# Low parts of the selecting stage's u tiles from an accumulating DMA instead of VectorE, heads of two engines unrolled

## The reference, cut to what matters

```python
q  = (h @ w_pq).reshape(b, s, PEER_HEADS, 2, PEER_HALF)          # 8 heads
sc = einsum('bshpc,pnc->bshpn', q, sub_keys)                     # 2 x 128 keys
top_v, top_i = lax.top_k(sc, 16)                                 # per half
cand = top_v[..., 0, :, None] + top_v[..., 1, None, :]
best_v, best_i = lax.top_k(cand, 16)
expert = i1 * 128 + i2                                           # of 16384 experts
gate = softmax(best_v)
a   = einsum('bthkd,btd->bthk', u_emb[expert], h)
out = einsum('bthk,bthkd->btd', gelu(a) * gate, v_emb[expert])
```

## Time and profile before

| | us |
|---|---|
| median of 3 runs | 4106.17 |
| lowest, highest | 4091.32, 4109.74 |
| the profiled execution's own time | 4093.63 |
| its span in the trace | 4091.9 |
| selecting, about | from 1657 to 2693 |

### The profile page before, as it was taken

One profiled execution on the slowest core, in us unless ns is written; L12 is line 12 of the kernel. 1 busy time (PEld: TensorE's weight loads), 2 busy tenths in 40 slices (PEclk: granted clock), 3 DMA queues, 4 the chain that ended last, 5 costly groups with the idle time before them and its releaser, 6 DMA issues. The chain is left out here.

```text
span 4091.9 us, 62946 instructions
## 1 busy us (share of the span) xinstructions
PE 3733.3 (91%) x21687; PEld 3298.7 (81%) x21687; DVE 3030.5 (74%) x5237; ACT 1466.2 (36%) x2548; POOL 1670.7 (41%) x1277
## 2 busy tenths in 40 slices
PE   6999999998899999799888889888886999999997
PEld 5776777775677877698888888888886999999996
DVE  5677777777753413469999999784463999999998
ACT  3455555566543433322222222233342222222222
POOL 2433434443212112025555555632222656566562
PEclk9999999998999999899999999989997999999998
DMA  2111111111343313158888888845448999999995
GB/s 86 44 52 47 52 41 48 47 50 65 123 181 113 113 36 115 53 190 309 307 290 317 316 316 308 320 173 219 167 152 329 387 390 389 387 391 387 388 391 201
DMA packets 316060, 848.09 MB, mean 207 GB/s; under 512 B 28752, under 2 KB 124240, under 8 KB 311888
## 3 DMA queue, kind: packets, MB, share of 16 engines
q1 hardware_dynamic: 202384, 400.92, 28.7%
q0 software_dynamic: 110592, 402.70, 25.9%
q10 hardware_dynamic: 2880, 41.94, 2.5%
HBM read 726.96 MB, written 118.49 MB: 207 GB/s over the span
## 5 line engine op out<-in xcount | busy, mean ns | idle before, releaser
L1922 POOL DMA_INDIRECT join_urow<-in_u_rows,select_row_now x384 | 510.8, 1330 | 510.7 <-issue 244.9
L2652 POOL DMA_INDIRECT spread_vrow<-in_v_rows,spread_row_of x384 | 543.3, 1415 | 379.3 <-DVE spread_y L2723 263.6
L163 PE MATMUL spread_banks<-spread_ahi,spread_vhi 128*128 128x384 f32 (+1 forms) x2048 | 638.0, 312 | 35.7 <-DVE spread_acc L2713 20.9
L163 PE MATMUL select_products<-h_hi,shared_pair_hi 128*128 128x256 f32 (+2 forms) x1728 | 575.6, 333 | 98.5 <-DVE shared_raw_low L1736 89.0
L164 PE MATMUL spread_banks<-spread_alo,spread_vhi 128*128 128x384 f32 (+1 forms) x2048 | 635.1, 310 | 0.0
L165 PE MATMUL spread_banks<-spread_ahi,spread_vlo 128*128 128x384 f32 (+1 forms) x2048 | 634.9, 310 | 0.0
L163 PE MATMUL shared_carry<-shared_wide_hi,shared_w_hi 128*128 128x512 f32 x1408 | 559.4, 397 | 28.6 <-DVE shared_wide_lo L591 11.2
L164 PE MATMUL select_products<-h_lo,shared_pair_hi 128*128 128x256 f32 (+2 forms) x1728 | 569.8, 330 | 2.8 <-issue 2.8
L165 PE MATMUL select_products<-h_hi,shared_raw_low 128*128 128x256 f32 (+2 forms) x1728 | 569.5, 330 | 2.2 <-issue 2.1
L164 PE MATMUL shared_carry<-shared_wide_lo,shared_w_hi 128*128 128x512 f32 x1408 | 554.8, 394 | 0.0
L165 PE MATMUL shared_carry<-shared_wide_hi,shared_w_lo 128*128 128x512 f32 x1408 | 554.4, 394 | 0.0
(11 more groups left out here) (304 smaller groups left out, 6911.9 us busy)
## 6 DMA issues: line engine op xcount, KB each, us to landing
spread_vraw<-in_peer_v SPq DMA_DIRECT2D x128, 512.0 KB
shared_raw<-in_select_pairs SPq DMA_DIRECT2D x104, 512.0 KB
gates<-spread_stage ACTq DMA_DIRECT2D x20, 2048.0 KB, 15.0
spread_act<-gelu_u SPq DMA_DIRECT2D x128, 320.0 KB
spread_graw<-gates SPq DMA_DIRECT2D x128, 320.0 KB
gelu_u<-front SPq DMA_DIRECT2D x92, 320.0 KB, 4.1
shared_w_raw<-in_w_mix SPq DMA_DIRECT2D x56, 512.0 KB, 3.6
join_uraw<-in_peer_u SPq DMA_DIRECT2D x36, 512.0 KB
```

What stands on the lines that cost most here:

```text
L163: nc.tensor.matmul(out, whi, xhi, start=(first and i == 0), stop=False)
L1922: nc.gpsimd.indirect_dma_start(picks.slots[s][:], None, u_rows, bass.IndirectOffsetOnAxis(row_now[:, t, j:j + 1], 0)).then_inc(row_loaded[ ...
L2652: nc.gpsimd.indirect_dma_start(v_slots[s][:], None, v_rows, bass.IndirectOffsetOnAxis(row_of[:, par, t, j:j + 1], 0)).then_inc(row_loaded[ ...
```

## The change

ScalarE, right behind the high part of a tile, also writes the negated high part into the low buffer. GpSimd then issues a second DMA of the same tile from memory, with an add: what lies in the low buffer (minus high) plus the tile, which is the low part. VectorE's subtraction is gone. TensorE waits for this DMA's semaphore instead of VectorE's. There is one semaphore for each slot, since several of these DMAs may be in flight.

GpSimd's program is written anew: each body now has one `low` for each tile, with the fetches of the head before distributed between them by the table `FETCHED` (8 behind the first, then 4 behind each, none behind the last), and the tail has one `low` with five fetches behind each. VectorE's and GpSimd's eight bodies are all written out, without a loop.

```diff
         self.nc.scalar.activation(self.hi[:, s], self.raw[:, s], ACT.Copy).then_inc(self.hi_made, 1)
-
-    def low(self, dve, x, s):
-        dve.wait_ge(self.hi_made, x + 1)
-        self.nc.vector.tensor_tensor(self.raw_low[:, s], self.raw[:, s], self.hi[:, s].bitcast(F32), ALU.subtract
-                                     ).then_inc(self.lo_made, 1)
+        act.wait_ge(self.hi_made, x + 1)
+        self.nc.scalar.activation(self.raw_low[:, s], self.hi[:, s].bitcast(F32), ACT.Copy, scale=-1.0).then_inc(self.turned, 1)
+
+    def low(self, pool, x):
+
+        pool.wait_ge(self.turned, x + 1)
+        self.nc.gpsimd.dma_start(self.raw_low[:, x % 4], self.pairs_in[x // 2, :, x % 2].rearrange("p c n -> p (c n)").bitcast(F32R),
+                                 accum_op=ALU.add).then_inc(self.low_loaded[x % 4], 16)
...
-        if h == 0:
-            pe.wait_ge(self.lo_made, x + 1)
+        if h == 0 and not (isinstance(x, int) and x < 4):
+            pe.wait_ge(self.low_loaded[s], turn * 16)
...
+            FETCHED = (0, 8, 12, 16, 20, 24, 28, 32, 36, 40, 44, 48, 48)
+
             def body(hd, first, last):
-                if not first:
-                    for k in range(PICKS):
-                        fetch(hd - 1, k)
-
-            heads(pool, body)
-            for k in range(PICKS):
-                fetch(PH - 1, k)
+                for j in range(2 * PAIRS_PER_HEAD):
+                    if not first or j >= 2:
+                        pr.low(pool, tile_of(hd, j)[0])
+                    if not first:
+                        for k in range(FETCHED[j], FETCHED[j + 1]):
+                            fetch(hd - 1, k)
+
+            for hd in range(PH):
+                body(hd, hd == 0, hd == PH - 1)
+            for j in range(2 * TAIL_PAIRS):
+                pr.low(pool, 2 * (N - TAIL_PAIRS) + j)
+                for k in range(5 * j, min(5 * j + 5, PICKS)):
+                    fetch(PH - 1, k)
...
-                low(0)
...
-            heads(dve, body)
+            for hd in range(PH):
+                body(hd, hd == 0, hd == PH - 1)
...
             for j in range(2 * TAIL_PAIRS):
-                tail_low(j)
                 dots(PH - 1, 4 * j, 4 * j + 4)
```

More of the change, by code:

```diff
@@ L1713, in __init__ @@
         self.loaded = [m.sem(f"tile_loaded{s}", start=16) for s in range(4)]
-        self.hi_made, self.lo_made = m.sem("tile_hi_made", start=4), m.sem("tile_lo_made", start=4)
+        self.hi_made, self.turned = m.sem("tile_hi_made", start=4), m.sem("tile_turned", start=4)
+        self.low_loaded = [m.sem(f"tile_low_loaded{s}") for s in range(4)]
         self.done = m.sem("product_done")
@@ L1752, in first_pair, with product @@
                     mm.then_inc(self.done, 1)
-    def product(self, pe, x, s, h, width):
-        if h == 0:
-            pe.wait_ge(self.lo_made, x + 1)
+    def product(self, pe, x, turn, s, h, width):
+        if h == 0 and not (isinstance(x, int) and x < 4):
+            pe.wait_ge(self.low_loaded[s], turn * 16)
         pe.wait_ge(self.read, x * 2 + (h - 3))
@@ L1980, in body @@
                 for j in range(2 * PAIRS_PER_HEAD):
-                    x, _, s = tile_of(hd, j)
+                    x, turn_of, s = tile_of(hd, j)
                     i = j // 2
                     for h in range(2):
-                        pr.product(pe, x, s, h, HALF[h] if kind_of(i, last) is None else H)
+                        pr.product(pe, x, turn_of, s, h, HALF[h] if kind_of(i, last) is None else H)
                         if h == 0 and j == 0 and first:
@@ L1993, in _ @@
                 for h in range(2):
-                    pr.product(pe, x, x % 4, h, HALF[h])
+                    pr.product(pe, x, x // 4, x % 4, h, HALF[h])
                 if j == 2:
@@ L2241, in some @@
                         dots(hd - 1, a, b)
[L2243 to L2246, removed]
                 alone(dve, sc_made, hd * 2 + 2)
@@ L2256, in body @@
                 some(3, 6)
-                low(1)
                 second_best(0, 16)
@@ L2262, in body @@
                 some(9, 12)
-                low(2)
                 find_second(8, 16)
@@ L2267, in body @@
                 some(12, 15)
-                low(3)
                 candidates()
@@ L2273, in body @@
                 some(18, 21)
-                low(4)
                 candidate_best(0, 8)
@@ L2279, in body @@
                 some(24, 27)
-                low(5)
                 candidate_cut(4, 8)
                 some(27, 30)
-                low(6)
                 if not first:
@@ L2288, in body @@
                 some(30, 33)
-                low(7)
                 alone(dve, clast8, hd * NT + NT)
@@ L2292, in body @@
                 some(33, 36)
-                low(8)
                 positions(hd)
@@ L2298, in body @@
                 some(39, 42)
-                low(9)
                 hits_halve(hd)
                 some(42, 45)
-                low(10)
                 hits_quarter(hd)
                 some(45, 48)
-                low(11)
                 hits_sum(hd)
@@ L2319, in turned_low @@
                                                ).then_inc(low_read, 1)
-            def tail_low(j):
-                x = 2 * (N - TAIL_PAIRS) + j
-                pr.low(dve, x, x % 4)
             for j in range(2 * TAIL_PAIRS):
-                tail_low(j)
                 dots(PH - 1, 4 * j, 4 * j + 4)
```

## The result

| | median us | range | runs |
|---|---|---|---|
| before | 4101.40 | 4091.32 to 4109.74 | 4 |
| changed | 4146.24 | 4142.14 to 4148.14 | 4 |

The ratio is 1.0109, 95% interval 1.0082 to 1.0136: about 45 us slower, in the direction forecast, with about half of the forecast size (+85 us on the profiled execution; the two profiled executions are 54.5 us apart).

The account below looks back on a forecast made before the run. VectorE was taken as the bound, the DMA engines becoming it after the change: +57 us for seven bodies, +10 start, +18 tail, +85 on the profiled 4093.6, so 4179, predicted as 4180 us; range 4045 to 4275.

Parts of the forecast that it names:

- What bounds: Selecting, bodies 0 to 6: VectorE bounds at 95% busy, 113.8 us a body; without its subtractions it could run 99.1.
- TensorE's floor of 102.0: Selecting: TensorE's busy time of 102.0 us a body, at clock 0.95, is the floor without any DMA trouble.
- The accumulate, 2.68 us: Each of a body's twelve accumulating DMAs costs two gathers' DMA time, 2.68 us, as it reads two sources.
- The body, 122 us: Selecting's seven bodies: 124.0 us of DMA time each, pace 118 to 124, taken as 122; 8.2 slower each, +57 us.
- the value stage's share of 1.05: Full DMA engines in the value stage show share 1.05, so a body could go as low as 124.0 / 1.05 = 118 us.
- The start, +10 us: Head 0: accumulates ahead of the first gather delay the first dot from 1805.1 to about 1815, +10 us; nothing gained.
- The tail, +18 us: Last head's 48 gathers: 88 us of DMA time become 115 with ten accumulates at 2.68, +18 us.
- ScalarE and GpSimd at nothing: Selecting: ScalarE's extra copies, 12.7 us a body, and GpSimd's twelve more issues, 20 us, fit under the others, costing nothing.
- A: Rival, chance 0.25: an accumulate costs what a gather costs, 1.34 us; body 106 us, total 4054.
- B: Rival, chance 0.15: a wash at 4100, from an accumulate of about 1.8 us or queue waits of 5 us a body.
- C: Rival, chance 0.15 with anything like it: an accumulate costs three passes, 4.0 us; body 140 us, total 4317.
- The written-out heads at nothing: VectorE's and GpSimd's unrolled bodies: less register work might save at most 6 us a body; counted as nothing.

Follow-up runs that it names:

- the plain copy: The changed kernel with the second DMA copying the same 512 KB without the add (low parts wrong); ratio to before 0.9917, body 109.4 us.
- order: The changed kernel with four gathers behind each of the twelve accumulates instead of eight behind the first; ratio to before 1.0126, body 120.4 us.
- half-width: The changed kernel with the accumulating DMA over the first half of the channels only, 256 KB; ratio to before 0.9874, body 109.2 us.
- GpSimd's subtractions: The kernel before, heads written out, with four or six of twelve low parts subtracted by GpSimd, the rest by VectorE; ratios 0.9994 and 1.0025.
- the three groups: The follow-up experiments fall into three groups, each run on a chip of its own, every ratio taken to the kernel before measured beside it.

## Why the prediction was right, point by point

The direction, the bound and its cause were right: the DMA engines full, VectorE and TensorE waiting for them. The size was not: up to the rows of body 7, +67 us were forecast and +22.7 came (17.4 of the 18 in the tail). Bodies 2 to 7 account for 30 of the missing 45 us (8.2 each forecast, 3.3 measured), head 0 for 12 and body 1 for 3. Term by term:

- **What bounds.** VectorE was the bound, and relieving it is worth much: 100.4 us a body without the second DMA, where 99.1 had been worked out for VectorE. TensorE's floor of 102.0 was too high. It was TensorE's busy time at a clock of 0.95; fed without gaps it got 0.99, and 97.5% of 100.4 is 97.9 us.
- **The accumulate, 2.68 us.** Right that it is well above a plain transfer, and dear as a size: 2.3 under load, 1.7 times a gather and not twice. The Trainium skill's "Collectives: The Full Stack", section "The bandwidth ceiling: the fold count and why AG ≠ RS ≠ AR", has a measured ratio of 1.93 for its collectives, put down to two source reads. That is above the 1.7 (under load) and 1.6 (quiet) measured here. By that ratio the prediction's sum would have been 8 us lower, an estimate from that page, where it says 7.
- **The body, 122 us.** This is the term that was mis-sized. The mean of seven is 118.6, and without the late gathers of body 1, which the forecast had put into the start, it is 117.2, just under the worked-out 118 to 124. Two things were off. The DMA time of a body is 119.3 us and not 124.0: counted by bytes, the 815 us hold seven bodies' transfers, 94.2 us a body on GpSimd's queue (forecast 96.5) and 25.1 on SyncE's (27.5). That the queue came so near was partly luck: its gathers were dearer, 66.1 for 64.3, and its accumulates cheaper, 27.9 for 32.2. And the engines ran at a share of 1.03, where 122 us for 124.0 had supposed 1.02: I took a pace inside the range instead of the end that the value stage's share of 1.05 pointed to.
- **The start, +10 us.** Wrong as put. Body 1 "at TensorE's pace, so nothing is gained" overlooked that TensorE itself waited for one of VectorE's low parts in head 0, 9.94 us, in the row of before below, a wait that the changed kernel does not have. Body 1 began 12.3 us earlier. The other half was right: the first gather came 9.7 us behind the copied scores (1795.0 against 1785.3), where 10 had been said. So the first dot began at 1804.5, as before at 1805.1, and not at 1815: what head 0 gained, the late gathers took back.

```profile
1736.34 0.69 PE L163 MATMUL select_products<-h_hi,shared_pair_hi 128*128 128x384 f32 x1 [9.94 <-DVE shared_raw_low L1736]
```

- **The tail, +18 us.** +17.4.
- **ScalarE and GpSimd at nothing.** Held: GpSimd is busy 60%; an accumulate's issue took 1.01 us of it (median), where 1.63 with the gap behind it had been assumed. ScalarE's copies took 1.06 us each, as assumed.
- **Rivals.** A's price, 1.34 for a plain transfer, is what the plain copy has (1.35), but the add costs 1.0 us more. B and C are out, by the order and half-width runs and by the price.
- **The written-out heads at nothing.** Alone they may be worth up to 0.6%. What they are worth in the changed kernel was not measured: it was not run with its loops kept.

## What to carry to other kernels

Before work is moved from a full engine to the DMA engines, add up their time in that stage as carefully as an engine's: their free seventh (16 us a body) was less than the bill (12 x 2.3, 28 us), though it looked idle next to VectorE's 95%. Price an accumulating DMA well above a plain one, here 1.6 to 1.7 times, and hold prices against each other only within one stretch or at one load. Count what a late start costs apart from the steady pace. And an idle engine is no free helper if its instructions hold up those of the full one: GpSimd's subtractions gave VectorE's time back as slower dots.

## What the runs showed of the hardware

- The DMA engines in a stage full of 512 KB transfers: 383 GB/s at a share of 1.00 with plain copies, 354 GB/s at 1.03 with every fifth transfer of GpSimd's an accumulate (the bytes that are added to are not in the 354).
- 512 KB took 1.92 us of the 16 engines' time as a plain copy and 3.0 as an accumulate in a quiet stretch, and 1.35 and 2.3 in full ones.
- TensorE's granted clock over 1800 to 2480 was 0.94 where it waited most (changed, busy 86%) and 0.99 where it hardly waited (no second DMA, 97.5%). In between it did not follow the busy time alone: 0.96 at 94% with the plain copy, 0.98 at 92% with the half width.
- The unchanged spreading stage took 1402 to 1434 us from run to run and chip to chip, as much as many a change is worth. It lay closer within two of the three groups (1402 to 1408, 1422 to 1430), but not in the first (1415 to 1434).
